# Raw weight blocks land in the remainder's ring slot and are split in place, two blocks ahead instead of three

## What is computed

```python
def reference(x, c, ctx, ...):          # all float32
    # first block
    hx = modulate(rmsnorm(x), ...);  ux = hx @ w_in          # same for the context
    ox = hgrn_bidir(...)                                     # gated linear scan, 4 heads
    x  = x + gate * merge_branches(ux, ox, w_a, w_b, w_out)
    h2 = modulate(rmsnorm(x), ...)
    z  = depthwise_3x3_conv(h2 @ ffn_up)                     # 5632 channels, on an 8 x 64 grid
    x  = x + gate * ((silu(z[..., :2816]) * z[..., 2816:]) @ ffn_down)
    # second block: retention (4 heads), swiglu, short convolution, swiglu
    for i in range(2):
        x = x + gate * (retention_mixer(...) if i == 0 else conv_mixer(...))
        x = x + gate * ((silu(f @ w1) * (f @ w3)) @ w2)
    return rmsnorm(x)
```

## Time and profile before

| | |
|---|---|
| median of 3 runs | 2486.67 us (2486.28 to 2488.55) |
| span of the profiled execution | 2489.8 us |
| mean granted TensorE clock | 0.973 of 2.4 GHz |
| TensorE matmul busy | 2344.0 us (94%) |
| VectorE busy | 1396.7 us (56%) |
| ScalarE busy | 868.3 us (35%) |
| GpSimd busy | 162.7 us (7%) |
| HBM traffic | 272 MB read, 110 GB/s over the span |

### The profile page before, as it was taken

The page is one execution under the profiler, slowest core; times in us unless marked ns, Lnnn a source line. Parts: engine busy times, 40 slices in busy tenths (PEclk is TensorE's granted clock), DMA queues, the critical chain, the costliest instruction groups (busy, mean ns, idle before and its releaser), DMA issues.

```text
span 2489.8 us, 29701 instructions
## 1 busy us (share of the span) xinstructions
PE 2344.0 (94%) x10264; PEld 1879.6 (75%) x10264; DVE 1396.7 (56%) x2054; ACT 868.3 (35%) x1160; POOL 162.7 (7%) x96
## 2 busy tenths in 40 slices
PE   7998889998999997999999987999998998999997
PEld 3887657877888786787877865888886886888885
DVE  4546645648999868475555546655524445333322
ACT  4433223325555333232323233444323223434322
POOL 0000000004666100000000000000000000000000
PEclk9999889999999998999999998999999999999999
DMA  6421105631333642323332321666632322323331
GB/s 261 136 76 43 34 34 161 194 118 59 101 95 96 191 151 78 117 76 104 98 110 83 116 86 52 211 193 189 183 94 68 105 90 68 110 93 101 100 94 51
DMA packets 72935, 274.99 MB, mean 110 GB/s; under 512 B 8096, under 2 KB 8480, under 8 KB 71328
## 3 DMA queue, kind: packets, MB, share of 16 engines
q1 hardware_dynamic: 53424, 199.74, 25.7%
q10 hardware_dynamic: 19440, 74.27, 9.4%
HBM read 271.88 MB, written 2.10 MB: 110 GB/s over the span
## 4 chain that ended last, share of the span: by engine, by line
PE 88%; DVE 6%; issue 3%; ACT 2%; DMA 1%; DVEq 0%; POOL 0%; ACTq 0%; SPq 0%
PE bank L390 82%; PE bank L775 1%; PE bank L853 1%; PE bank L695 1%; DVE rstd L438 1%; DVE rt L1691 1%; DVE hx_lo L446 1%; DVE tnorm L453 0%; DVE rstd L1561 0%; PE bank L801 0%; ACT w_hi L341 0%; DVE rv_lo L1732 0%; PE bank L421 0%; PE bank L423 0%; DMA ident<-in_ident 0%
## 5 line engine op out<-in xcount | busy, mean ns | idle before, releaser
L390 PE MATMUL bank<-hx_hi,w_hi 128*128 128x512 f32 x1792 | 712.1, 397 | 40.1 <-DVE hx_lo L446 35.0
L390 PE MATMUL bank<-hx_lo,w_hi 128*128 128x512 f32 x1792 | 706.4, 394 | 0.0
L390 PE MATMUL bank<-hx_hi,w_lo 128*128 128x512 f32 x1792 | 705.6, 394 | 0.0
L349 DVE TENSOR_TENSOR w_lo<-w_raw,w_hi 128x1024 fp32r<-128x1024 f32 x306 | 374.8, 1225 | 534.3 <-ACT w_hi L341 527.2
L341 ACT ACTIVATE w_hi<-w_raw 128x1024 fp32r<-128x1024 f32 x350 | 369.0, 1055 | 487.5 <-PE bank L390 446.2
L390 PEld LDWEIGHTS bank<-hx_hi,w_hi 128*128 128x128 f32 x1792 | 341.7, 191 | 117.1 <-issue 40.8
L390 PEld LDWEIGHTS bank<-hx_hi,w_lo 128*128 128x128 f32 x1792 | 341.5, 191 | 72.6
L390 PEld LDWEIGHTS bank<-hx_lo,w_hi 128*128 128x128 f32 x1792 | 341.7, 191 | 70.8 <-issue 0.9
L1620 DVE SCALAR_TENSOR_TENSOR bank<-zpad,cols,bank 128x512 f32<-128x512 f32 x352 | 233.8, 750 | 11.3 <-ACT bank L1237 11.1
L390 PE MATMUL bank<-hid_hi,w_hi 128*128 128x512 f32 x528 | 209.3, 396 | 1.5 <-POOL hid_lo L1876 1.5
L390 PE MATMUL bank<-hid_hi,w_lo 128*128 128x512 f32 x528 | 210.4, 399 | 0.0
(11 more groups left out here) (289 smaller groups left out, 2762.2 us busy)
## 6 DMA issues: line engine op xcount, KB each, us to landing
w_raw<-in_wstream SPq DMA_DIRECT2D x350, 512.0 KB, 3.6
ada_raw<-in_ada_nk ACTq DMA_DIRECT2D x128, 512.0 KB, 3.7
ada_w<-in_ada_kn SPq DMA_DIRECT2D x8, 1024.0 KB, 18.8
dec<-in_dec ACTq DMA_DIRECT2D x4, 960.0 KB, 4.8
x_tok<-in_x SPq DMA_DIRECT2D x1, 2048.0 KB, 7.8
dft<-in_dft ACTq DMA_DIRECT2D x1, 2048.0 KB, 7.7
out_x<-out_tok SPq DMA_DIRECT2D x4, 512.0 KB, 2.6
crow<-in_crow SPq DMA_DIRECT2D x3, 512.0 KB, 23.2
```

The source lines that it names most:

```text
L349: nc.vector.tensor_tensor(w_lo[nb.at % RING][:], w_raw[nb.at % RAW][:], w_hi[nb.at % RING][:].bitcast(F32), ALU.subtract).then_inc(lo_read ...
L390: ins = nc.tensor.matmul(out_ap, s, m, start=first and at == 0, stop=last and at == n - 1)
```

## The change

The landing buffers are gone. A raw block is loaded straight into the memory of its `w_lo` slot, of which there are four; `w_raw[s]` and `w_lo[s]` are two names (float32 and float32r) for the same bytes, and the remainder overwrites the raw values in place. A slot of `w_lo` is free for a load only when TensorE is done with the block in it, so SP waits for `block_done` of block n - 4 instead of `lo_ready` of block n - 2, and ACT's own wait for `block_done` in `split_hi` goes. The splits run two blocks ahead instead of three: the call at block b now makes block b + 2. At the start four blocks are loaded instead of two, ahead of the last three pieces of `ada_w0`, and the split of block 2, which stood alone ahead of the first stage, is gone from there.

```diff
-RAW = 2
-AHEAD = RING - 1
+EARLY = 2
+AHEAD = RING - 2
...
-        w_raw = [sb(f"w_raw{s}", [P, BLK]) for s in range(RAW)]
         w_hi = [sb(f"w_hi{s}", [P, BLK], F32R) for s in range(RING)]
-        w_lo = [sb(f"w_lo{s}", [P, BLK], F32R) for s in range(RING)]
+        r_lo = [region(4 * BLK) for s in range(RING)]
+        w_raw = [sb(f"w_raw{s}", [P, BLK], F32, r_lo[s]) for s in range(RING)]
+        w_lo = [sb(f"w_lo{s}", [P, BLK], F32R, r_lo[s]) for s in range(RING)]
...
-            act.wait_ge(raw_ready[nb.at % RAW], nb.loads())
-            if nb.at >= RING:
-                act.wait_ge(block_done, nb.count(1 - RING))
-            nc.scalar.activation(w_hi[nb.at % RING][:], w_raw[nb.at % RAW][:], ACT.Copy).then_inc(hi_ready, 1)
+            act.wait_ge(raw_ready[nb.at % RING], nb.loads())
+            nc.scalar.activation(w_hi[nb.at % RING][:], w_raw[nb.at % RING][:], ACT.Copy).then_inc(hi_ready, 1)
...
-            with sp.Fori(0, N_BLOCKS // RAW - 1) as i:
-                for s in range(RAW):
-                    n = i * RAW + (s + RAW)
-                    sp.wait_ge(lo_ready, i * RAW + (s + 1))
+            with sp.Fori(0, N_BLOCKS // RING - 1) as i:
+                for s in range(RING):
+                    n = i * RING + (s + RING)
+                    sp.wait_ge(block_done, i * RING + (s + 1))
                     sp.dma_start(w_raw[s][:], wstream[bass.ds(n, 1)].rearrange("o p n -> (o p) n"))\
                         .then_inc(raw_ready[s], 16)
...
-            for b in range(RAW):
+            for b in range(EARLY):
                 split_hi(act, Block(b - AHEAD))
...
-            for b in range(RAW, AHEAD):
+            for b in range(EARLY, AHEAD):
                 split_hi(act, Block(b - AHEAD))
```

More of the change, by code:

```diff
@@ L98, in loads @@
     def loads(self):
-        first = 16 * (self.at // RAW + 1)
-        return first if self.i is None else self.i * (16 * self.per // RAW) + first
+        first = 16 * (self.at // RING + 1)
+        return first if self.i is None else self.i * (16 * self.per // RING) + first
 def program(nc, wstream, ada_kn, ada_nk, x_in, ctx1_in, ctx2_in, cols_in, crow_in, ident_in, masks_in,
@@ L261, in program @@
         acc = [[bw[0], bank[4]], [bw[1], bn]]
-        raw_ready = [sem(f"raw_ready{s}") for s in range(RAW)]
+        raw_ready = [sem(f"raw_ready{s}") for s in range(RING)]
         hi_ready, lo_ready, block_done = sem("hi_ready"), sem("lo_ready"), sem("block_done")
@@ L348, in split_lo @@
             dve.wait_ge(hi_ready, nb.count(1))
-            nc.vector.tensor_tensor(w_lo[nb.at % RING][:], w_raw[nb.at % RAW][:],
+            nc.vector.tensor_tensor(w_lo[nb.at % RING][:], w_raw[nb.at % RING][:],
                                     w_hi[nb.at % RING][:].bitcast(F32), ALU.subtract).then_inc(lo_ready, 1)
@@ L573, in _ @@
             sp.dma_start(masks[:], masks_in).then_inc(masks_landed, 16)
-            with sp.Fori(0, N_BLOCKS // RAW - 1) as i:
-                for s in range(RAW):
-                    n = i * RAW + (s + RAW)
-                    sp.wait_ge(lo_ready, i * RAW + (s + 1))
+            with sp.Fori(0, N_BLOCKS // RING - 1) as i:
+                for s in range(RING):
+                    n = i * RING + (s + RING)
+                    sp.wait_ge(block_done, i * RING + (s + 1))
                     sp.dma_start(w_raw[s][:], wstream[bass.ds(n, 1)].rearrange("o p n -> (o p) n"))\
                         .then_inc(raw_ready[s], 16)
+            for n in range(N_BLOCKS // RING * RING, N_BLOCKS):
+                sp.wait_ge(block_done, n - RING + 1)
+                sp.dma_start(w_raw[n % RING][:], wstream[n]).then_inc(raw_ready[n % RING], 16)
             for t in range(LT):
@@ L1862, in split @@
                 pool.wait_ge(hi_ready, nb.count(1))
-                nc.gpsimd.tensor_tensor(w_lo[nb.at % RING][:], w_raw[nb.at % RAW][:],
+                nc.gpsimd.tensor_tensor(w_lo[nb.at % RING][:], w_raw[nb.at % RING][:],
                                         w_hi[nb.at % RING][:].bitcast(F32), ALU.subtract).then_inc(lo_ready, 1)
```

## The result

| | before | after |
|---|---|---|
| median | 2487.6 us (2486.3 to 2493.2, 4 runs) | 2521.2 us (2518.9 to 2521.9, 4 runs) |
| ratio, 95% interval | | 1.0132 (1.0119 to 1.0146) |
| span of the profiled execution | 2489.8 us | 2520.1 us |

The change costs 1.3%. The forecast was 2513 us, its range 2494 to 2524.

The account below looks back on a forecast made before the run. TensorE, 88% of the chain, was taken to bound the kernel, with splits late at a few places. The terms sum to +26.4 us, taking the median from 2486.7 to 2513 us; the 8-in-10 range was 2494 to 2524.

Parts of the forecast that it names:

- term 4: Retention head 0: TensorE idles 7 us ahead of block 124, replacing most of a 6.76 us wait; +3.7 us, up to 6.
- Term 1: Up stage: POOL's split behind its product comes 0.55 us late, 20 times, +0.94 us each with the restart; +18.8 us.
- Term 2: Start of the up stage: POOL's first split, now block 58, ends after TensorE wants it; +0.8 us.
- Term 3: Start of the down stage: DVE's first split, now block 102, is late for TensorE; +3.0 us, bounds 2.4 and 5.
- Term 5: Starts of the two swiglus: the split is late at B and just in time at A; +1.0 us for both.
- Term 6: First stage: ACT's lone split goes and the work up to TensorE's release moves up; -0.9 us.
- In place: Splits overwriting the raw block: no change in split time; 0.1 us either way in POOL's would move the up-stage cost 2 us.
- Loads don't decide: All blocks: a load takes a median of 3.6 us and ACT's split comes at least 5.4 us after its start.
- the split in time: Rival, up stage: the chain is over 0.6 us shorter, so its cost goes and 7.6 us are left; 2494 us, 8%.
- the faster case: Rival, retention heads: DVE's chains begin earlier and TensorE's waits shrink by up to 17 us; 2469 us, 4%.
- The deeper load ring is none: Rival, two swiglus: loads waiting for TensorE come late, costing 0.3 us a block in 88 blocks; 2539 us, 3%.
- The clock falls in the up stage: Rival, up stage: frequent new waits lower TensorE's clock, 1.3 us lost a pair; 2539 us, 7%.

Follow-up runs that it names:

- E2: Kernel before, its landing buffers and loads released by the splits kept, with splits two blocks ahead instead of three; 2516.2 us, 1.0114.
- E1: Changed kernel with both of POOL's splits ahead of its gating product in the up stage, instead of one on each side; 2498.2 us, 1.0033.
- E5: Kernel before with the lone split of block 2 moved ahead of the copies of the first stage's modulation rows; 2489.2 us, 0.9996.
- E3: Changed kernel, in place with the ring of four, but with splits three blocks ahead instead of two; 2531.0 us, 1.0177.
- E9: Kernel before with ACT's split in the stage of the levels moved behind the first two level_k copies of a block; 2480.5 us, 0.9970.
- E6: Kernel before with DVE's splits of blocks 127 and 128 in head 0 moved behind the last rotation; 2485.0 us, 0.9990.

## Why the prediction was right, and where its sizes were off

The direction, the mechanism and the places held; the median lies 8 us above the forecast, inside the range. Only 1.1 us of the 8 lie from block 58 on, where term 4 was 2.5 too low and the others a little too high. The rest is what one set of executions differs by from another. In E2, which has the same cost from block 58 on in its trace, two of four executions took 2513.3 us, the forecast to within 1 us, and two took 6 to 9 us more. So where in its range the time fell is in part luck.

- **Term 1, up stage**: +18.8 forecast. The 20 odd blocks from 61 to 99 end 0.90 to 0.96 us later each, 18.6 in all. The wait that was to be "about 0.9 us each" shows as 0.62 us of idle time; the restart makes up the rest of the 0.93. E1 takes it away, E2 has it without the rest of the change. DVE stayed hidden, as said.
- **Term 2, start of up**: +0.8; block 58 ends 0.55 us later.
- **Term 3, start of down**: +3.0; block 102's part measured +3.1, of which 0.7 came back at the next block, where TensorE would have waited for the context's transfer. Net +2.4, the lower bound: the half clock feared behind the wait came (granted 0.50 over 848.3 to 855.1), but the kernel before has 6.8 us of it at this place too (828.9 to 835.7), so it cost nothing more.
- **Term 4, head 0**: +3.7 forecast, "up to 6 if the clock is low behind both waits". It measured +6.2 (block 124 +9.6, block 126 -3.4), since both were followed by low clock: granted 0.51 over 995 to 1002 and 0.52 over 1019 to 1026, with first matmuls of 0.80 and 0.77 us. This is the term that was mis-sized: I took the new wait of 7 us as free of that price though the old one of 6.76 us had it. The wait of 7.37 us cost its length and 2.2 us more, with a granted 0.50 over the 4.1 us from 997.8 to 1001.9.
- **Term 5, swiglus**: +1.0; block 286 +0.8, block 188 nothing.
- **Term 6, first stage**: -0.9; the path gives 0.95 (E5). In the profile it is -3.1, the rest being the clock, which comes and goes (granted 0.86 over 78 to 90 before, 1.00 after, 0.86 in E1 with the same code as after).
- **In place**: no change forecast; DVE's split takes 1225 ns in both, POOL's 2405 before and 2407 after.

From block 58 on the terms add up to 27.3 us, and the trace has 28.4. The 2.9 us missing ahead of it (+2.0 against -0.9), and the 3.3 us by which the medians differ more (33.6) than the spans (30.3), are the clock's chance between executions as far as the runs tell; that the change makes the unlucky pattern more frequent isn't excluded.

The sentence that fell is one of the rule's supports: "Loads don't decide". It is true two ahead, where ACT stands 377.8 us for transfers and none of it reaches TensorE. It is false three ahead in place (E3). Even two ahead the reason given, that ACT asks for block n only behind the end of block n - 3, 5.4 us after its load began, doesn't hold everywhere: 92 times ACT came to its split before the block had landed. In the down stage ACT was ready for block 107 at 863.24 us, 0.87 us before block 103 ended and the load could start:

```profile
868.95 1.06 ACT L340 ACTIVATE w_hi<-w_raw 128x1024 fp32r<-128x1024 f32 x1 [5.71 <-DMA w_raw<-in_wstream]
```

TensorE came to block 107 only at 881.34. So what kept loads from deciding was the distance to TensorE, not that ACT asks late. I had costed AHEAD and the ring as separate parts, and they are one.

Of the rivals, the split in time is refuted by the 20 waits, and the faster case by the column 127 to 283, +0.2 us where heads 1 to 3 should have gained. *The deeper load ring is none*: ACT's waits for transfers did grow, from 38.9 to 377.8 us, but no block from 186 to 251, swiglu A and its down projection, became longer by more than 0.02 us. *The clock falls in the up stage* is refuted by one row, a wait of 0.62 us (with the slower restart 0.93 us) every 11.8 us at a granted 1.00:

```profile
584.00:830.00 246.00, 232.47 (x998) 185.83 (x999) 220.45 (x332) 126.39 (x188) 150.75 (x83) 1.00 0.30 92
```

The stage of the levels shows the other side: waits of 2.3 us every 13 us go with a granted 0.88, of 1.3 us every 10.7 us with 1.00 (E9). The Trainium skill, "TensorE: Matmul & The Clock Gate", section on a second failure mode (psum-queue depth-cycling), tells of a kernel in which TensorE's micro-idles between groups of matmuls were frequent enough to make the clock swing between its levels. The stage of the levels agrees with that, its clock going between a granted 1.00 and 0.50; in the up stage, idles as frequent but shorter left the clock at 1.00.

## What to carry to other kernels

A pipeline depth is a position in every engine's list: lowering it by one moves no instruction and yet makes each produce the block before, so look for the one place per loop and per stage start where the producer stands behind work that follows from its consumer. Such a cost can be mended by order at the same depth: here three small moves gave back 31 us in the traces. And when a buffer is shared by load, split and use, ask in whose list the wait for the load stands and what is queued behind it, since in E3 ACT's 3 us of standing still in each block of one stage became 24 us of TensorE over eight blocks.

## What the runs showed of the hardware that I had not expected

- Whether TensorE's clock is full in the stretch of state updates differs from one execution to the next, and moves the end of block 24 by up to 8.9 us (between E6 and the change; 7.7 between E1 and the change, which run the same code up to there). Its groups of eight 128-column matmuls, first after the change, then in E1:

```profile
314.24 2.07 PE L803 MATMUL bank<-v_x,kd_x 128*128 128x128 f32 x8 [0.69 <-ACT kd_x L1177]
```

```profile
314.15 1.16 PE L803 MATMUL bank<-v_x,kd_x 128*128 128x128 f32 x8 [0.69 <-ACT kd_x L1177]
```

  The waits ahead of them are the same 0.69 us; the groups take 2.07 us at a granted 0.50 and 1.16 at 1.00. I found no cause. Executions of the kernel before spread over 14 us (2483.3 to 2497.4 in all batches).
- Shortening a wait by 1 us (2.3 to 1.3, E9) was worth up to 2.5 us a block, because the half clock behind it went as well.
